# Gate and up products of an FFN by seven block products in place of eight, with sums of weight blocks formed on GpSimd

## Chip, cores and metric

The kernel runs on one core of a Trainium2 chip. The metric is the device time of one execution in microseconds (us), and shorter is better. TensorE (PE) multiplies matrices, VectorE (DVE) and ScalarE (ACT) work element by element, GpSimd (POOL) did little but issue transfers, and SyncE (SP) issues the loads of the big weights.

## The reference

Ten sublayers in a row over one sequence of 256 tokens with 1024 features, all in float32: an attention mixer, FFN, a Fourier mixer, FFN, then twice (FFN, token mixer, FFN). Six of the ten are FFNs, and the change touches these alone:

```python
def swiglu_2(h, w_in, w_out):
    gate, up = jnp.split(h @ w_in, 2, axis=-1)
    return (jax.nn.silu(gate) * up) @ w_out
```

`h` is the normed and modulated input, 256 x 1024. `w_in` holds gate and up weights, 1024 x 2816 each; `w_out` is 2816 x 1024. Each sublayer has a modulation (shift, scale, gate) which is a vector of 3072 numbers, the product of one row of 1024 numbers with a 1024 x 3072 matrix.

## The kernel before

**Layout.** Features lie on the partitions: `h` is 8 tiles of 128 x 256 (features x tokens). A weight tile of 128 x 128 is stationary in TensorE and the 256 tokens of `h` move through. One float32 matmul of the program shows as two records of MATMUL in the trace, so a count in a row is twice the count of the code's `mm` calls.

**An FFN.** The 2816 hidden features are 22 tiles. Tile n is unit n of the phase `w13`: gate (8 matmuls over the 8 feature tiles) and up (8 more) into the two halves of one PSUM bank `lin[n % 3]`. Two units come from one load of 2 MB (a block of `w13`, 11 to an FFN), 32 matmuls a block. ScalarE takes Silu of the gate half (L835), VectorE multiplies it by the up half and writes `big[:, n]` (L1422), features on the partitions, as the second product wants it. Then the phase `w2` makes 8 tiles of the result, 22 matmuls each (`project`), with VectorE adding each to `x` (`residual`, L1012).

In five of the six FFNs (sublayers 1, 3, 6, 7, 9, `folded`) the first 4 units (`RAW`) are made from the input before its norm is known (`raw_unit`), and VectorE scales them afterwards (`raw_scaled`, then L1416). From unit 4 on all six run alike, through `pairs`. Sublayer 4 runs all its units through `pairs`.

**Loads.** SyncE fills a ring of three slots of 2 MB, `ring`; a slot is loaded again when `s_unit` says that the units of its last block are summed.

**Modulation.** The matrices of later sublayers' modulations come in blocks of 0.5 MB (`ada`). GpSimd issues their loads (L464) into a ring of three slots, each after VectorE has used up the block three before (`s_ada_used`); VectorE reduces a block with one multiply-and-sum (L871). `ADA_PER_FFN` fixes how many blocks each FFN takes: 48, 48, 32, 32, 32, 0. Five eighths of them are spread over units 2 to 21, three eighths over the results of `w2`. This is VectorE's program order, written by hand:

```python
def ada(n):
    for _ in range(n):
        dve.wait_ge(s_ada_dma[m % ADA_SLOTS], ...)
        V.tensor_tensor_reduce(w, w, crow[...], ...).then_inc(s_ada_used, 1)
```

**Between the products.** TensorE waits for VectorE's multiply of unit 21 (`pe.wait_ge(*taken(unit0[s, "w2"] - 1))`) before the first matmul of `w2`.

**The engines' order.** Each engine executes its own list in order. A wait on a semaphore holds everything behind it on that engine.

Of the kernel before, what the change touches and what calls it, by code (L numbers as in the profile page):

```python
# [16 lines left out]
ALU = mybir.AluOpType  # L17
# [45 lines left out]
ADA_PER_FFN = [48, 48, 32, 32, 32, 0]  # L63

# [32 lines left out]
def build(nc, I, out, stop=10, dbg=None):  # L97
    subs = SUBS[:stop]
    with ExitStack() as ctx:
# [3 lines left out]
        def sem(name):  # L103
            return ctx.enter_context(nc.semaphore(name))
# [140 lines left out]
        s_squares_added = sem("squares_added")  # L245
        s_mixer_tables_dma = sem("mixer_tables_dma")
# [137 lines left out]

        def first_weights(n):
# [70 lines left out]
        def _(pool):  # L456
# [4 lines left out]
            for n in range(ADA_N * len(subs) - FIRST_GATE):  # L461
                if n >= ADA_SLOTS:
                    pool.wait_ge(s_ada_used, n - ADA_SLOTS + 1)
                pool.dma_start(ada_ring[n % ADA_SLOTS][:], I["ada"][n]).then_inc(s_ada_dma[n % ADA_SLOTS], 16)  # L464
# [3 lines left out]
        def _(act):  # L468
# [317 lines left out]
            for s, kind in enumerate(subs):  # L786
# [36 lines left out]
                if kind == "ffn":  # L823
                    u0 = unit0[s, "w13"]
                    for n in range(KF):
# [25 lines left out]
        def _(dve):  # L851
# [26 lines left out]
            def ffn_before(s):  # L878

                return subs[:s].count("ffn")  # L880
# [122 lines left out]
            def residual(s, name):  # L1003
# [6 lines left out]
                for m in range(KD):  # L1010
# [8 lines left out]
                    if name == "w2":  # L1019
                        ada(share(ADA_PER_FFN[ffn_before(s)] * 3 // 8, KD - 2, m))  # L1020
# [347 lines left out]
            for s, kind in enumerate(subs):  # L1368
# [37 lines left out]
                if kind == "ffn":  # L1406

                    ffn = subs[:s].count("ffn")
                    u0 = unit0[s, "w13"]
                    for n in range(KF):  # L1410
                        if folded(s) and n < RAW:
# [3 lines left out]
                            dve.wait_ge(s_silu, ffn * KF + n + 1)  # L1415
# [4 lines left out]
                        else:  # L1420
                            dve.wait_ge(s_silu, ffn * KF + n + 1)
# [14 lines left out]
        def _(pe):  # L1436
# [486 lines left out]
            for s, kind in enumerate(subs):  # L1923
# [15 lines left out]
                if kind == "ffn":  # L1939
# [166 lines left out]
```

## Time and profile before

| | |
|---|---|
| median of 3 runs | 2274.36 us (2272.35 to 2275.43) |
| the profiled execution | 2274.54 us |
| its span, first to last instruction | 2272.5 us |
| TensorE busy (matmul records) | 2211.6 us, 97% |
| VectorE, ScalarE, GpSimd busy | 34%, 16%, 5% |
| transfers | 438.27 MB, mean 193 GB/s |
| mean granted TensorE clock | 0.987 of full speed |

Times are those of one profiled execution. The 2.0 us between its span and its time are start and end of the program. "Busy" of a matmul group is the time covered by its records; the mean ns of one record is longer than the step from one to the next, because records overlap. "Idle before" is the time in which the engine did nothing just before instructions of the group, with what ended it.

### The profile page before, as it was taken

The page shows a single profiled execution, that of the slowest core. Times are in us where ns is not written, and L with a number is a line of the kernel's source. Part 1 is how long each engine was busy: PE and PEld are TensorE (multiplying, and loading weights), DVE is VectorE, ACT ScalarE, POOL GpSimd, SP SyncE. Part 2 cuts the span into 40 slices and gives each one's busy share as a digit, 9 for nine tenths or more (in the row PEclk, how much of TensorE's full clock was granted, in tenths as well). Part 3 has the DMA queues.
Part 4 walks back from the last instruction along what each step waited for, and adds up shares of the span by engine and source line. Part 5 has one row for each costly group of instructions (what it writes and reads, how often), then busy time and mean ns, then how long its engine had stood idle before and what let it go on. Part 6 is the DMA issues. An engine that isn't in the chain of part 4 may idle for free.

```text
span 2272.5 us, 23963 instructions
## 1 busy us (share of the span) xinstructions
PE 2211.6 (97%) x10232; PEld 1871.7 (82%) x10232; DVE 766.8 (34%) x1601; ACT 356.2 (16%) x667; POOL 118.8 (5%) x231
## 2 busy tenths in 40 slices
PE   7999999999999999999999999999999999999997
PEld 4777888868888888888788888888888868888886
DVE  6454333313334122336433422332233543340002
ACT  3233200022000100023140200020002223120001
POOL 0100011100111000100000000000010000000000
PEclk9999999999999999999999999999999999999998
DMA  9673576825767565643434465656564433444331
GB/s 357 226 259 102 213 267 245 311 79 186 270 248 295 220 230 199 254 147 146 162 111 148 157 231 200 236 195 231 213 231 154 154 148 111 148 148 148 137 127 70
DMA packets 61539, 438.27 MB, mean 193 GB/s; under 512 B 6976, under 2 KB 8768, under 8 KB 39552
## 3 DMA queue, kind: packets, MB, share of 16 engines
q1 hardware_dynamic: 28608, 318.35, 38.4%
q0 software_dynamic: 32256, 117.45, 13.9%
q8 instruction: 75, 1.23, 0.2%
q10 hardware_dynamic: 576, 1.05, 0.1%
q14 instruction: 24, 0.20, 0.0%
HBM read 434.72 MB, written 2.10 MB: 192 GB/s over the span
## 4 chain that ended last, share of the span: by engine, by line
PE 97%; DVE 1%; ACT 1%; issue 0%; DMA 0%; SPq 0%; ACTq 0%; DVEq 0%
PE lin L1460 79%; PE small_ps L1460 4%; PE lin L1775 2%; PE lin L1718 1%; PE small_ps L1794 1%; PE lin L1528 1%; PE lin L1732 1%; PE small_ps L1564 1%; PE small_ps L1685 1%; PE lin L1672 1%; PE lin L1740 1%; PE small_ps L1766 0%; PE pstat L1472 0%; PE lin L1600 0%; PE small_ps L1615 0%; PE lin L1587 0%
## 5 line engine op out<-in xcount | busy, mean ns | idle before, releaser
L1460 PE MATMUL lin<-h,ring 128*128 128x256 f32 x5424 | 1180.3, 380 | 5.4 <-ACT h L807 2.8
L1460 PEld LDWEIGHTS lin<-h,ring 128*128 128x128 f32 x5424 | 1030.0, 190 | 150.7 <-issue 9.2
L1460 PE MATMUL lin<-big,ring 128*128 128x256 f32 x2112 | 457.4, 379 | 7.9 <-DVE big L1422 7.9
L1460 PEld LDWEIGHTS lin<-big,ring 128*128 128x128 f32 x2112 | 400.8, 190 | 64.5 <-DVE big L1422 10.3
L871 DVE CUSTOM_DVE_ANT_0 ada_ring<-ada_ring,crow 128x1024 f32<-128x1024 f32 x224 | 268.2, 1219 | 26.7 <-DMA ada_ring<-in_ada 26.1
L1422 DVE TENSOR_TENSOR big<-sil,lin 128x256 f32<-128x256 f32 x112 | 47.1, 421 | 592.8 <-ACT sil L835 592.8
L464 POOL DMA_DIRECT2D ada_ring<-in_ada x224 | 118.3, 528 | 1592.9 <-DVE sums L871 1561.0
L1012 DVE SCALAR_TENSOR_TENSOR x<-lin,mod,x 128x256 f32<-128x256 f32 x80 | 38.7, 483 | 449.3 <-PE lin L1460 424.2
L835 ACT ACTIVATE sil<-lin 128x256 f32<-128x256 f32 x112 | 42.9, 383 | 723.2 <-PE lin L1460 723.2
L1460 PE MATMUL lin<-rec,ring 128*128 128x257 f32 (+1 forms) x608 | 148.2, 397 | 7.8 <-ACT rec L532 7.8
L1460 PEld LDWEIGHTS lin<-rec,ring 128*128 128x128 f32 x608 | 120.8, 199 | 28.5 <-issue 9.6
L1460 PE MATMUL small_ps<-rec,ring 128*128 128x257 f32 x448 | 102.0, 379 | 0.0
L1460 PEld LDWEIGHTS small_ps<-rec,ring 128*128 128x128 f32 x448 | 84.9, 189 | 12.5
L532 ACT ACTIVATE rec<-xc,modc 128x256 f32<-128x256 f32 x40 | 16.5, 496 | 353.8 <-DVE xc L934 353.8
L1775 PE MATMUL lin<-ring,h 128*128 128x512 f32 x128 | 56.7, 595 | 0.0
L1775 PEld LDWEIGHTS lin<-ring,h 128*128 128x128 f32 x128 | 23.7, 190 | 28.3 <-issue 28.3
L1304 DVE RECIPROCAL rec<-rec 128x1024 f32<-128x1024 f32 x2 | 13.1, 6552 | 55.9 <-ACT rec L775 55.9
L1321 DVE TENSOR_TENSOR att<-lin,big 128x512 f32<-128x512 f32 x16 | 11.1, 691 | 56.8 <-PE lin L1460 56.8
L1460 PE MATMUL lin<-yab,ring 128*128 128x256 f32 x128 | 30.2, 379 | 0.0
L1000 DVE RECIPROCAL rstd<-sd 128x256 f32<-128x256 f32 x10 | 17.5, 1753 | 33.1 <-ACT sd L508 33.1
L478 ACT ACTIVATE big<-lin 128x512 f32<-128x512 f32 x24 | 14.3, 596 | 89.4 <-PE lin L1460 80.6
L545 ACT ACTIVATE h<-xc,modc 128x256 f32<-128x256 f32 x56 | 28.2, 585 | 0.0
(296 smaller groups left out, 1175.1 us busy)
## 6 DMA issues: line engine op xcount, KB each, us to landing
ring<-in_w SPq DMA_DIRECT2D x66, 2048.0 KB, 8.3
ada_ring<-in_ada POOLq DMA_DIRECT2D x224, 512.0 KB, 5.6
ring<-in_w SPq DMA_DIRECT2D x48, 1408.0 KB, 6.1
ring<-in_gates SPq DMA_DIRECT2D x12, 2048.0 KB, 7.9
ring<-in_mproj SPq DMA_DIRECT2D x8, 2048.0 KB, 8.0
ring<-in_mtok SPq DMA_DIRECT2D x4, 2048.0 KB, 7.7
ring<-in_branch SPq DMA_DIRECT2D x4, 2048.0 KB, 7.8
ring<-in_wout SPq DMA_DIRECT2D x4, 2048.0 KB, 7.8
```

The source lines that it names most:

```text
L464: pool.dma_start(ada_ring[n % ADA_SLOTS][:], I["ada"][n]).then_inc(s_ada_dma[n % ADA_SLOTS], 16)
L545: A(h[:, k], xc[:, k], ACT.Identity, scale=fold_gain[:, k:k + 1], bias=fold_shift[:, k:k + 1]).then_inc(s_h_ready, 1)
L835: A(sil[:, n % 2], lin[(u0 + n) % NBANK][:, 0:T], ACT.Silu).then_inc(s_silu, 1)
L871: V.tensor_tensor_reduce(w, w, crow[:, 0 if s < FIRST2 else 1], 1.0, 0.0, ALU.mult, ALU.add, sums[:, s % 3, b:b + 1]).then_inc(s_ada_used, 1)
L1012: V.scalar_tensor_tensor(x[:, m], lin[(u0 + m) % NBANK][:, 0:T], mod[:, 16 + m:17 + m], x[:, m], ALU.mult, ALU.add).then_inc(s_taken_by_dv ...
L1422: V.tensor_tensor(big[:, n], sil[:, n % 2], lin[(u0 + n) % NBANK][:, T:2 * T], ALU.mult).then_inc(s_taken_by_dve, 1)
L1460: ins = mm(dst, w[:, lo:lo + m], rhs(k), start=k == 0, stop=k == nk - 1)
L1528: ins = mm(lin[i // 2][0:2, i % 2 * T:i % 2 * T + T], csil[:, 0:2, k], first_weights(n)[:, k * T:(k + 1) * T], start=k == 0, stop=k == KD - 1)
L1564: return nc.tensor.transpose(dst, src, ident[:])
L1672: mm(lin[n % NBANK][:], q, kh[:, a], start=True, stop=True).then_inc(s_logits, 1)
L1685: ins = mm(dst, vt[:, k, a * VD:(a + 1) * VD], pt[:, k], start=k == 0, stop=k == 3)
L1775: ins = mm(b[:], h[:, k, tt * P:tt * P + P], w[:, k * 512:(k + 1) * 512], start=k == 0, stop=k == KD - 1)
```

## The change

Tiles 0 to 3 of each FFN stay as they were. The other 18 tiles are made in 9 chunks of two tiles (one 2 MB block each), by a scheme that gets a product of 2 x 2 blocks from seven block products in place of eight. The 256 tokens are two halves, the 1024 features two halves, and the columns are the gate columns and the up columns of the chunk's two tiles. With A(i,k) for the quarters of `h` and B(k,j) for those of the weights, VectorE forms four sums of A once per FFN (`combine_h`), and GpSimd four sums of B in each chunk (`combine`: t1 = B12-B11, t2 = B22-t1, t3 = B22-B12, t4 = B21-t2, each 128 x 1024 elements).

Each of the seven products is 4 matmuls (`part`). Here a 128 x 128 tile of `h` or of its sums is stationary, and 256 columns of weights move; the result has tokens on its partitions. It lies in seven PSUM banks (`product_bank`). ScalarE copies two products to SBUF, VectorE makes nine operations of 128 x 256 a chunk out of the rest (`chunk`), and ScalarE applies Silu. Since `w2` wants features on the partitions, TensorE turns the hidden values with four 128 x 128 transposes a chunk (`turn_hidden`), and ScalarE copies them to `big`.

GpSimd now has the sums of weights and the issue of the modulation's loads in one list, with the loads of a chunk between t2 and t3. The modulation's blocks are placed anew: some before the first chunk, then 3, 3, 2, 2, 2, 0 after each chunk and after each of six results of `w2`. The first tile of `w2` begins before the last chunk's hidden values are turned.

```diff
+ADA_PER_CHUNK = [3, 3, 2, 2, 2, 0]
+ADA_PER_RESULT = [3, 3, 2, 2, 2, 0]
+CHUNKS = KF // 2 - RAW // 2
...
+def ada_before_chunks(f):
+    return ADA_IN_MLA + sum(ADA_PER_FFN[:f + 1]) - CHUNKS * ADA_PER_CHUNK[f] - (KD - 2) * ADA_PER_RESULT[f]
...
+def combined_weights(j, i):
+    place = ((proj[:, 0:4], proj[:, 4:8], proj[:, 8:12], proj[:, 12:16]),
+             (proj[:, 16:20], proj[:, 20:24], tok[:, 0:1], tok[:, 1:2]))[j % 2][i]
+    return place.rearrange("p a b -> p (a b)").rearrange("p (u kf) -> p u kf", u=2)
...
+def product_bank(s, n):
+    after = unit0[s, "w2"]
+    place = {1: pa[2], 2: pa[1], 3: pa[3], 5: pa[0], 6: lin[after % NBANK], 7: lin[(after + 1) % NBANK],
+             4: lin[(after + 2) % NBANK]}
+    return place[n][:, 0:T]
...
+    ada_issued = [0]
+    def ada_issue(used):
+        while ada_issued[0] < min(used + ADA_SLOTS, ADA_N * len(subs) - FIRST_GATE):
+            n = ada_issued[0]
+            ada_issued[0] += 1
+            if n >= ADA_SLOTS:
+                pool.wait_ge(s_ada_used, n - ADA_SLOTS + 1)
+            pool.dma_start(ada_ring[n % ADA_SLOTS][:], I["ada"][n]).then_inc(s_ada_dma[n % ADA_SLOTS], 16)
+    def combine(ph, f, j):
+        n, done = ph.first + RAW // 2 + j, f * CHUNKS + j - 1
+        if j >= 2:
+            pool.wait_ge(s_fourth_product, done)
+        pool.wait_ge(s_weights[n % SLOTS], (n // SLOTS + 1) * 16)
+        b11, b12, b21, b22 = [quarter(n % SLOTS, c, half) for half in range(2) for c in range(2)]
+        t1, t2, t3, t4 = [combined_weights(j, i) for i in range(4)]
+        W = nc.gpsimd.tensor_tensor
+        W(t1, b12, b11, ALU.subtract).then_inc(s_weights_combined, 1)
+        pool.wait_ge(s_weights_combined, nth(pool, s_weights_combined))
+        W(t2, b22, t1, ALU.subtract).then_inc(s_weights_combined, 1)
+        ada_issue(ada_before_chunks(f) + max(j - 1, 0) * ADA_PER_CHUNK[f])
+        W(t3, b22, b12, ALU.subtract).then_inc(s_weights_combined, 1)
+        pool.wait_ge(s_weights_combined, nth(pool, s_weights_combined))
+        W(t4, b21, t2, ALU.subtract).then_inc(s_weights_combined, 1)
+        nth(pool, s_weights_combined, 2)
+    for s, kind in enumerate(subs):
+        if kind == "ffn":
+            f = ffn_before(s)
+            ada_issue(ADA_IN_MLA + sum(ADA_PER_FFN[:f]))
+            pool.wait_ge(s_unit, unit0[s, "w13"] + 1)
+            for j in range(CHUNKS):
+                combine(by_name[s, "w13"], f, j)
+    ada_issue(ADA_N * len(subs))
...
+            for j in range(CHUNKS + 1):
+                if j < CHUNKS:
+                    act.wait_ge(s_first_product, nth(act, s_first_product))
+                    if j:
+                        act.wait_ge(s_first_up, nth(act, s_first_up))
+                    A(first_kept, product_bank(s, 1), ACT.Copy).then_inc(s_first_kept, 1)
+                if j:
+                    act.wait_ge(s_second_gate, nth(act, s_second_gate))
+                    A(second_gate, second_gate, ACT.Silu).then_inc(s_second_gate_silu, 1)
+                    act.wait_ge(s_hidden_turned, nth(act, s_hidden_turned))
+                    at = RAW + 2 * (j - 1)
+                    A(big[:, at:at + 2], pstat[:].rearrange("p (a b) -> p a b", a=2), ACT.Copy).then_inc(s_hidden_kept, 1)
+                if j < CHUNKS:
+                    act.wait_ge(s_first_gate, nth(act, s_first_gate))
+                    A(first_gate, first_gate, ACT.Silu).then_inc(s_first_gate_silu, 1)
+                    act.wait_ge(s_fifth_product, nth(act, s_fifth_product))
+                    if j:
+                        act.wait_ge(*taken(u0 + RAW + 2 * (j - 1) + 1))
+                    A(fifth_kept, product_bank(s, 5), ACT.Copy).then_inc(s_fifth_kept, 1)
+            nth(act, s_first_up)
...
+    def combine_h(s):
+        dve.wait_ge(s_h_ready, KD * (s + 1))
+        a11, a12, a21, a22 = [quarter_of_h(half, tt) for tt in range(2) for half in range(2)]
+        s1, s2, s3, s4 = [combined_h(i) for i in range(4)]
+        V.tensor_tensor(s1, a21, a22, ALU.add).then_inc(s_h_combined, 1)
+        V.tensor_tensor(s3, a11, a21, ALU.subtract).then_inc(s_h_combined, 1)
+        dve.wait_ge(s_h_combined, nth(dve, s_h_combined))
+        V.tensor_tensor(s2, s1, a11, ALU.subtract).then_inc(s_h_combined, 1)
+        dve.wait_ge(s_h_combined, nth(dve, s_h_combined, 2))
+        V.tensor_tensor(s4, a12, s2, ALU.subtract).then_inc(s_h_combined, 1)
+        nth(dve, s_h_combined)
+    def chunk(s, j):
+        def added(dst, a, b, signal=s_dve_chain):
+            V.tensor_tensor(dst, a, b, ALU.add).then_inc(signal, 1)
+            dve.wait_ge(signal, nth(dve, signal))
+        dve.wait_ge(s_second_product, nth(dve, s_second_product))
+        dve.wait_ge(s_first_kept, nth(dve, s_first_kept))
+        V.tensor_tensor(first_gate, product_bank(s, 2), first_kept, ALU.add).then_inc(s_first_gate, 1)
+        dve.wait_ge(s_sixth_product, nth(dve, s_sixth_product))
+        added(partial_2, product_bank(s, 6), first_kept)
+        dve.wait_ge(s_fifth_kept, nth(dve, s_fifth_kept))
+        if j:
+            dve.wait_ge(s_hidden_turned, nth(dve, s_hidden_turned))
+        added(first_up, partial_2, fifth_kept)
+        added(first_up, product_bank(s, 3), first_up, s_first_up)
+        dve.wait_ge(s_first_gate_silu, nth(dve, s_first_gate_silu))
+        V.tensor_tensor(first_up, first_up, first_gate, ALU.mult).then_inc(s_taken_by_dve, 1)
+        dve.wait_ge(s_seventh_product, nth(dve, s_seventh_product))
+        added(partial_3, product_bank(s, 7), partial_2)
+        dve.wait_ge(s_fourth_product, nth(dve, s_fourth_product))
+        V.tensor_tensor(second_gate, product_bank(s, 4), partial_3, ALU.add).then_inc(s_second_gate, 1)
+        added(partial_3, partial_3, fifth_kept)
+        dve.wait_ge(s_second_gate_silu, nth(dve, s_second_gate_silu))
+        V.tensor_tensor(second_gate, partial_3, second_gate, ALU.mult).then_inc(s_taken_by_dve, 1)
+        if j == CHUNKS - 1:
+            nth(dve, s_hidden_turned)
...
-                ada(share(ADA_PER_FFN[ffn] * 5 // 8, KF - 2, n - 2) if n > 1 else 0)
+                if n == 2:
+                    combine_h(s)
+            ada(ada_before_chunks(ffn) - ada_blocks[0])
+            for j in range(CHUNKS):
+                chunk(s, j)
+                ada(ADA_PER_CHUNK[ffn])
...
+    def gate_and_up(s):
+        ph, f = by_name[s, "w13"], ffn_before(s)
+        u0, before = ph.unit0, ffn_before(s) * CHUNKS
+        def part(product, activation, weight):
+            out = product_bank(s, product).rearrange("p (u f) -> p u f", u=2)
+            for k in range(4):
+                ins = mm(out, activation[:, k], weight[:, :, k * P:(k + 1) * P], start=k == 0, stop=k == 3)
+            return ins
+        def turn_hidden(j):
+            pe.wait_ge(*taken(u0 + RAW + 2 * j + 1))
+            if j:
+                pe.wait_ge(s_hidden_kept, before + j)
+            for a in range(2):
+                for tt, tokens in enumerate((first_up, second_gate)):
+                    at = a * T + tt * P
+                    ins = turn(pstat[:, at:at + P], tokens[:, a * P:(a + 1) * P])
+            ins.then_inc(s_hidden_turned, 1)
+        h_tile(KD - 1)
+        pe.wait_ge(s_h_combined, 4 * (f + 1))
+        for j in range(CHUNKS):
+            n = ph.first + RAW // 2 + j
+            slot_of(ph, 0, RAW // 2 + j)
+            b11, b12, b21, b22 = [quarter(n % SLOTS, c, half) for half in range(2) for c in range(2)]
+            t1, t2, t3, t4 = [combined_weights(j, i) for i in range(4)]
+            if j:
+                pe.wait_ge(s_first_gate, before + j)
+            else:
+                pe.wait_ge(*taken(u0 + 2))
+            part(1, quarter_of_h(0, 0), b11).then_inc(s_first_product, 1)
+            part(2, quarter_of_h(1, 0), b21).then_inc(s_second_product, 1)
+            if j:
+                turn_hidden(j - 1)
+                pe.wait_ge(s_first_up, before + j)
+            pe.wait_ge(s_weights_combined, 4 * (before + j + 1))
+            part(3, combined_h(3), b22).then_inc(s_unit, 2)
+            if j:
+                pe.wait_ge(s_fifth_kept, before + j)
+                pe.wait_ge(s_second_gate, before + j)
+            else:
+                pe.wait_ge(*taken(u0 + RAW - 1))
+            part(5, combined_h(0), t1).then_inc(s_fifth_product, 1)
+            part(6, combined_h(1), t2).then_inc(s_sixth_product, 1)
+            part(7, combined_h(2), t3).then_inc(s_seventh_product, 1)
+            part(4, quarter_of_h(1, 1), t4).then_inc(s_fourth_product, 1)
+        last = CHUNKS - 1
+        ph = by_name[s, "w2"]
+        w = slot_of(ph, 0, 0)
+        b = bank(ph.unit0)
+        def result(k0, k1):
+            for k in range(k0, k1):
+                if k >= RAW and k % 2 == 0:
+                    pe.wait_ge(s_hidden_kept, before + (k - RAW) // 2 + 1)
+                ins = mm(b[:, 0:T], w[:, k * P:(k + 1) * P], big[:, k], start=k == 0, stop=k == KF - 1)
+            return ins
+        pe.wait_ge(s_first_up, before + CHUNKS)
+        result(0, 16)
+        turn_hidden(last)
+        result(16, KF).then_inc(s_unit, 1)
...
-            for b in range(RAW // 2 if folded(s) else 0, ph.nb):
-                pairs(ph, b // SLOTS, b % SLOTS, 2, h_tile)
-            pe.wait_ge(*taken(unit0[s, "w2"] - 1))
-            project(s, "w2", lambda k: big[:, k])
+            if not folded(s):
+                for b in range(RAW // 2):
+                    pairs(ph, b // SLOTS, b % SLOTS, 2, h_tile)
+            gate_and_up(s)
+            ph = by_name[s, "w2"]
+            for m in range(1, KD):
+                w = slot_of(ph, m // SLOTS, m % SLOTS)
+                tile_sum(bank(ph.unit0 + m)[:, 0:T], w, 0, KF, lambda k: big[:, k]).then_inc(s_unit, 1)
```

## Rows read from the trace of the kernel before

**Rows 1.** The page: busy time and share of the span by engine; chain that ended last
```profile
PE 2211.6 (97%) x10232; PEld 1871.7 (82%) x10232; DVE 766.8 (34%) x1601; ACT 356.2 (16%) x667; POOL 118.8 (5%) x231
...
PE 97%; DVE 1%; ACT 1%; issue 0%; DMA 0%; SPq 0%; ACTq 0%; DVEq 0%
```

**Rows 2.** Chain in order of time (start us, us, what): FFN of sublayer 1, units 4 to 21, then w2
```profile
255.33 124.33 PE lin L1460 x576
380.92 76.24 PE lin L1460 x352
```

**Rows 3.** The chain between unit 21 and w2 in sublayer 1
```profile
379.66 0.02 issue
379.68 0.02 ACTq L834
379.70 0.04 issue
379.74 0.39 ACT sil L835
380.14 0.02 issue
380.16 0.43 DVE big L1422
380.59 0.33 issue
```

**Rows 4.** Chain elsewhere: transposes (L1564), 512 moving columns (L1775), 128 moving columns (L1794)
```profile
129.43 1.75 PE small_ps L1564 x16
...
1075.36 6.87 PE lin L1775 x16
...
1082.23 1.78 PE small_ps L1794 x16
```

**Rows 5.** Windows (units 4 to 21; w2): PE, PEld, DVE, ACT, POOL, PEclk, DMA share, GB/s
```profile
255.33:379.66 124.33, 124.32 (x576) 109.09 (x575) 39.41 (x76) 7.02 (x18) 14.25 (x27) 1.00 0.70 256
380.92:457.16 76.24, 76.24 (x353) 67.15 (x354) 26.02 (x48) 1.89 (x3) 10.56 (x20) 1.00 0.77 291
```

**Rows 6.** Groups of the whole trace on VectorE (busy us, mean ns | idle before)
```profile
L871 DVE CUSTOM_DVE_ANT_0 ada_ring<-ada_ring,crow 128x1024 f32<-128x1024 f32 x224 | 268.2, 1219 | 26.7 <-DMA ada_ring<-in_ada 26.1
...
L1422 DVE TENSOR_TENSOR big<-sil,lin 128x256 f32<-128x256 f32 x112 | 47.1, 421 | 592.8 <-ACT sil L835 592.8
...
L1234 DVE TENSOR_TENSOR xc<-rec 128x1024 f32<-128x1024 f32 x2 | 2.4, 1218 | 0.0
```

**Rows 7.** Groups of the whole trace on GpSimd: all that it writes itself, and its issues
```profile
L464 POOL DMA_DIRECT2D ada_ring<-in_ada x224 | 118.3, 528 | 1592.9 <-DVE sums L871 1561.0 <-DMA rec<-in_ada_pe 32.0
L457 POOL MEMSET ones<- 128x128 f32 x1 | 0.2, 205 | 0.3 <-POOLq L2097 0.3
...
L458 POOL MEMSET eps<- 128x1 f32 x1 | 0.1, 98 | 0.0
```

**Rows 8.** Timeline of sublayer 1 around unit 3's end (255.33): VectorE's chain to the first modulation block
```profile
257.23 0.48 DVE L1416 SCALAR_TENSOR_TENSOR big<-rec,small,sil 128x256 f32<-128x256 f32 x1 [0.98 <-ACT sil L830]
257.63 1.22 DVE L871 CUSTOM_DVE_ANT_0 ada_ring<-ada_ring,crow 128x1024 f32<-128x1024 f32 x1
258.78 0.08 DVE L871 DVE_READ_ACCUMULATOR2_ANT sums<- 128x1 f32 x1
258.78 1.22 DVE L871 CUSTOM_DVE_ANT_0 ada_ring<-ada_ring,crow 128x1024 f32<-128x1024 f32 x1
259.15 0.53 POOL L464 DMA_DIRECT2D ada_ring<-in_ada  x1 [6.71 <-DVE sums L871]
```

**Rows 9.** Windows, columns as in Rows 5: an idle stretch of TensorE and the stretch behind it
```profile
986.06:989.40 3.34, 0.70 (x3) 0.33 (x3) 2.69 (x7) 0.66 (x2) 0.00 (x0) 1.00 0.52 167
989.40:994.80 5.40, 5.40 (x17) 4.44 (x18) 1.62 (x3) 5.38 (x12) 0.00 (x0) 0.68 0.01 3
```

**Rows 10.** ScalarE: a copy of 512 columns out of PSUM, and where function tables are loaded
```profile
L478 ACT ACTIVATE big<-lin 128x512 f32<-128x512 f32 x24 | 14.3, 596 | 89.4 <-PE lin L1460 80.6 <-PE lin L1732 8.9
...
L508 ACT ACT_TABLE_LOAD x9 | 11.5, 1283 | 0.2
...
L830 ACT ACT_TABLE_LOAD x5 | 6.4, 1283 | 0.1
```

More of the change, by code:

```diff
@@ L245, in build @@
         s_squares_added = sem("squares_added")
+        s_weights_combined = sem("weights_combined")
+        s_h_combined = sem("h_combined")
+        s_first_product = sem("first_product")
+        s_second_product = sem("second_product")
+        s_fourth_product = sem("fourth_product")
+        s_fifth_product = sem("fifth_product")
+        s_sixth_product = sem("sixth_product")
+        s_seventh_product = sem("seventh_product")
+        s_first_kept = sem("first_product_kept")
+        s_fifth_kept = sem("fifth_product_kept")
+        s_first_gate = sem("first_gate")
+        s_first_gate_silu = sem("first_gate_silu")
+        s_first_up = sem("first_up")
+        s_second_gate = sem("second_gate")
+        s_second_gate_silu = sem("second_gate_silu")
+        s_hidden_turned = sem("hidden_turned")
+        s_hidden_kept = sem("hidden_kept")
         s_mixer_tables_dma = sem("mixer_tables_dma")
@@ L383, in raw_pair, with ffn_before, quarter, combined_h @@
             return rec[:, 12 + 2 * (r % 2):14 + 2 * (r % 2)]
+        def ffn_before(s):
+            return subs[:s].count("ffn")
+        def ada_before_chunks(f):
+            return ADA_IN_MLA + sum(ADA_PER_FFN[:f + 1]) - CHUNKS * ADA_PER_CHUNK[f] - (KD - 2) * ADA_PER_RESULT[f]
+        def quarter(slot, c, half):
+            return ring[slot][:].rearrange("p (u c k f) -> p u c (k f)", u=2, c=2, k=KD)[:, :, c, half * 512:half * 512 + 512]
+        def combined_weights(j, i):
+            place = ((proj[:, 0:4], proj[:, 4:8], proj[:, 8:12], proj[:, 12:16]),
+                     (proj[:, 16:20], proj[:, 20:24], tok[:, 0:1], tok[:, 1:2]))[j % 2][i]
+            return place.rearrange("p a b -> p (a b)").rearrange("p (u kf) -> p u kf", u=2)
+        def combined_h(i):
+            return sq[:, 2 * i:2 * i + 2].rearrange("p a b -> p (a b)").rearrange("p (k t) -> p k t", k=4)
+        def quarter_of_h(half, tt):
+            return h[:, 4 * half:4 * half + 4, tt * P:tt * P + P]
+        first_kept, fifth_kept, partial_2, partial_3, first_gate, first_up, second_gate = [att[:, i] for i in range(7)]
+        def product_bank(s, n):
[3 more added lines that the diff above has]
+            return place[n][:, 0:T]
         def first_weights(n):
@@ L460, in _ @@
             pool.wait_ge(s_ada_first_dma[FIRST_N - 1], 16)
[L461 to L464, printed above, removed]
+            ada_issued = [0]
[30 more added lines that the diff above has]
+            ada_issue(ADA_N * len(subs))
         @block.scalar
@@ L824, in _ @@
                     u0 = unit0[s, "w13"]
-                    for n in range(KF):
+                    f = ffn_before(s)
+                    for n in range(RAW):
                         if n >= 2:
@@ L1019, in residual @@
                     if name == "w2":
-                        ada(share(ADA_PER_FFN[ffn_before(s)] * 3 // 8, KD - 2, m))
+                        ada(ADA_PER_RESULT[ffn_before(s)] if m < KD - 2 else 0)
                 dve.wait_ge(*taken(u0 + KD - 1))
@@ L1406, in _ @@
                 if kind == "ffn":
-                    ffn = subs[:s].count("ffn")
+                    ffn = ffn_before(s)
                     u0 = unit0[s, "w13"]
-                    for n in range(KF):
+                    for n in range(RAW):
                         if folded(s) and n < RAW:
@@ L1414, in _ @@
                             dve.wait_ge(s_raw_scaled, nth(dve, s_raw_scaled))
-                            dve.wait_ge(s_silu, ffn * KF + n + 1)
+                            dve.wait_ge(s_silu, ffn * RAW + n + 1)
                             V.scalar_tensor_tensor(big[:, n], raw_pair(n)[:, 1], raw_shift(n, 1), sil[:, n % 2],
```

4 lines of the change are left out of this document (1 added, 3 removed).

## The prediction

> **What bounds the kernel now.** I read the page first: TensorE is busy 97% of the span and is 97% of the chain that ended last [rows 1]. So only what changes TensorE's list, or makes it wait, counts. Then the chain in order of time, at one FFN: units 4 to 21 run without a gap, 576 records in 124.33 us, or 0.216 us a record, and `w2` the same (352 records in 76.24 us) [rows 2]. A matmul of the code is two records, 0.432 us; a block of two tiles is 64 records, 13.8 us. The windows confirm it: TensorE has no idle time in either stretch, at full clock, with weight loads (PEld 109 of 124 us) under the matmuls [rows 5]. Between the two stands one gap of 1.26 us (379.66 to 380.92): Silu, multiply, and 0.33 us until TensorE starts [rows 3].
>
> **Part 1, the products.** Each chunk loses 4 of 32 matmuls of 256 columns, 8 records: 8 x 0.216 = 1.73 us. Over 9 chunks x 6 FFNs, **-93.2 us**. That weights move now changes no price: 16 records of 512 columns over stationary activations took 6.87 us [rows 4], 0.215 us for 256 columns. The moving operand is now two pieces of 128 columns, which no row shows; I take it at nothing, since one operand is read at the same width either way.
>
> **Part 2, the transposes.** Four a chunk. The trace has transposes at 16 records in 1.75 us and plain 128-column matmuls, with all 128 columns stationary, at 1.78 us [rows 4]: 0.111 us a record. 54 x 8 x 0.111 = **+48.0 us**. The floor is 0.109; the ceiling is a weight load of 109.09/575 = 0.190 us a record [rows 5] should loads not overlap, +82 us. I take 0.111: those rows ran back to back.
>
> **Part 3, the gap before `w2`.** The last chunk's chain now has 16 matmuls (6.9 us) of `w2` over it, and ScalarE's copy (0.60 us [rows 10]) of the turned values has four more. Six gaps of 1.26 us: **-7.6 us**.
>
> **Part 4, the turn in the steady chunk.** Let 0 be the end of a chunk's fourth product. TensorE goes on at once with products 1 and 2 of the next, 16 records, and is ready to turn at 3.29 (its records end 0.16 us after the next one begins). Against it runs a chain: ScalarE must first copy the next first product (end of the record 1.73, then 0.08 to start, 0.38), only then Silu (0.39), then VectorE's multiply 0.43 and 0.33 to TensorE [rows 3]: 1.73 + 0.08 + 0.38 + 0.02 + 0.39 + 0.02 + 0.43 + 0.33 = 3.4. I put 0.08 us on each of 48 turns, **+3.8 us**. ScalarE's two kinds of function don't alternate tables: loads stand on the lines of Sqrt and of the first Silu behind it, none on a copy [rows 10]. There is little slack here, so whatever holds VectorE moves TensorE.
>
> **Part 5, the first chunk.** Here the code makes a wait that nothing covers. Between t2 and t3 of chunk 0 GpSimd issues loads of modulation blocks, and each waits for a block to be used. VectorE uses these (3 in the first two FFNs, 2 in the next three, none in the last) only after unit 3's multiply. Product 3 waits for t4. From unit 3's end: multiply at +1.90, first block at +2.30, each further block 1.15 later, its load's issue 1.52 behind the block's start and 0.53 long [rows 8], then t3 and t4. For 3 blocks: 2.30 + 2.30 + 1.52 + 0.53 + 0.2 for the two handovers + 2T, less the 3.46 us of products 1 and 2: 3.39 + 2T. For 2 blocks 2.24 + 2T; in sublayer 4, whose multiply comes 0.5 after the unit, 0.79 + 2T. In all 12.05 + 10T.
>
> **T, one sum of 128 x 1024 on GpSimd**, has no row. VectorE does it in 1.22 us [rows 6]. GpSimd's own rows are memsets: 128 columns 0.205, one column 0.098 [rows 7], so 0.84 ns a column for one stream, 0.96 us for 1024. With two inputs and one output: 1.8 us if two streams take turns, 2.7 if three do. I take 2.3, between these; ends 0.96 and 2.7. Part 5 is then **+35.0 us** (21.7 to 39.1). For this size the Trainium skill (GPSIMD Engine Reference, Performance versus the Vector engine) gives 4497 ns for 2048 elements, 2.25 us for ours as an estimate; no row here shows it, and the sum by it would be 0.5 us less.
>
> After idle time TensorE's clock is lower for a while: 3.34 us nearly idle, then 5.40 us at a mean of 0.68 (part at the 1.2 GHz level), for 16 records that at full clock take 16 x 0.217 = 3.5, while the 1.26 us gap is followed by full clock (2.4 GHz) [rows 5, 9]. Five stalls of 5 to 8 us at 1.9: **+9.6 us**.
>
> Parts 1 to 5: -93.2 + 48.0 - 7.6 + 3.8 + 35.0 + 9.6 = **-4.4 us**. The saving is nearly spent before anything steady goes wrong.
>
> **Part 6, GpSimd's steady list.** A chunk takes TensorE 56 x 0.216 + 0.89 + 0.08 = 13.04 us. In it GpSimd needs 4T = 9.2 plus issues; alone it would fit, since a chunk's three issues end at 7.3 after the fourth product and t3, t4 at 11.9. But GpSimd and VectorE read the same memory, and VectorE has four operations a chunk with both inputs there (0.42 each) and the blocks (1.15 each). No row has both at work on such operands: GpSimd only issued loads, and those took 0.528 us whether VectorE was busy or not. My forecast is that they take turns, each waiting only its share: t1 and t2 4.6, 0.84 for two of VectorE's adds, a block amid them 1.15; the other two blocks then end at 8.9, the last issue at 9.8, and t3, t4 with 0.84 more give 15.2 us. With 2 blocks it is 14.1, with none 10.9. GpSimd then falls behind. Its first free chunk (9.4) and seven at 15.2 make 115.8 against TensorE's 8 x 13.04 = 104.3: 11.5 us in each of two FFNs; 9.4 + 7 x 14.1 - 104.3 = 3.8 in each of three. **+34.4 us**; ends 0 and the rival of full holding.
>
> **What costs nothing.** `combine_h`: four adds of 512 columns, some 2.8 us, behind unit 2, under unit 3's 6.9 us; uncovered it would cost that once an FFN. VectorE's nine operations replace two a block: 3.8 + 3.5 us of blocks, in 13. The transfers: a block and three modulation blocks are 3.7 MB in 13 us, 283 GB/s, and `w2` ran without a stall at 291 [rows 5]; a slot is freed at product 3, two chunks before its next block is needed.
>
> **Sum.** -4.4 + 34.4 = +30.0 on the profiled execution's 2274.54 (span 2272.5 and 2.0 around it), which is the median of 2274.36 within 0.2: **2304.5 us**.
>
> **Rivals.**
> - *No interference* (the other side). GpSimd's and VectorE's reads pass each other, part 6 is 0: 2274.5 - 4.4 = 2270.1. With T at 0.96 it is 2256.8, at 2.7 2274.1. It decides at T = 2.3: below it the kernel is faster. For it: 0.528 us issues beside busy VectorE. Against: issues read no tensor. Chance 0.29, of which 0.18 is faster by over 0.2%.
> - *Full holding at the turn.* An operation of either engine keeps the other's two-input operation out for its whole length. Then in part 4 VectorE's last multiply, ready at 2.6, meets t2, which runs from about 2.85 (t1 to 2.4, then VectorE's add) to 5.15. The turn begins at 5.15 + 0.43 + 0.33 = 5.9, not 3.3: 2.6 us x 48 = 125 us. Such a chunk is 15.6 us and hides GpSimd's 15.2, so part 6 goes: -4.4 - 3.8 + 125 = +117, **2391 us**. Against it: it needs GpSimd to start t1 before VectorE's add, 0.4 us after the product; if VectorE is first, the turn waits some 0.6 us and the blocks push GpSimd: about 2315, inside the forecast's part. Chance 0.25.
> - *Transposes at the weight loads' pace*: the ceiling of part 2, +34 on the forecast, 2339. Against it: both rows of part 2. Chance 0.05. This is the case in which fewer products bring no shorter work.
> - Forecast, shares of a conflict between nothing and full: 0.35, mostly 2280 to 2325. Rest 0.06, half of it faster.
>
> The page rule of the second rival is that of the Trainium skill (SBUF — State Buffer, Who interferes with whom): a VectorE instruction with two SBUF inputs contends with a GpSimd instruction that reads SBUF, and the later one waits for the whole of the earlier. It speaks against this change, and no run here shows it yet. By it the time is 2391; by the rows alone nothing excludes either it or the first rival.
>
> **Numbers.** The range reaches from the middle of the first rival to just past the second: 2260 to 2398. Outside lie T near 1 us, and stalls of 2.6 us that also lower the clock. Within 0.2% (4.5 us, about what a measurement of this kernel can tell from no change) is a third of the first rival: 0.10. Faster 0.21, slower 0.69.
>
> **What the next profile would show.** Parts 1 and 2: MATMUL records of `part` at 0.216 us a step, transposes at 0.11. Part 5: idle time of TensorE at product 3 of chunk 0 of 5 to 8 us in five FFNs, none in the last, released by GpSimd, with the clock below 1 after it. Part 6: waits at product 3 of later chunks, released by GpSimd, growing with the blocks per chunk and absent in the last FFN. The second rival: 48 waits of about 2.6 us before the transposes, released by VectorE, in the last FFN too. T: GpSimd's groups. If TensorE's idle time at chunk 0 is missing, or GpSimd's sums take under 1.5 us, I am wrong toward faster.

## The result, and the profile after

The kernel with the change takes 2346.51 us (median of 4 runs, 2344.92 to 2347.92) against 2274.89 before: ratio 1.0317, 95% interval [1.0299, 1.0334]. It is 72 us slower, where +30 was forecast. Line numbers (L...) shift by a few from run to run with the edits.

The page of the changed kernel, against [rows 1]:

```profile
span 2344.8 us, 24735 instructions
PE 2171.7 (93%) x10016; PEld 1823.1 (78%) x10016; DVE 1161.1 (50%) x2003; ACT 428.2 (18%) x829; POOL 630.5 (27%) x447
...
PE 82%; DVE 14%; issue 2%; POOL 1%; ACT 1%; DMA 0%; SPq 0%; DVEq 0%; ACTq 0%
```

TensorE is busy 39.9 us less (2211.6 to 2171.7), but idle 112.2 us more: 2344.8 - 2171.7 = 173.1, where it was 60.9. VectorE's busy time has grown by 394 us, and VectorE now holds 14% of the chain. Who TensorE waited for (us in total, times, longest):

```profile
PE pstat L1716 <- DVE att L1025: 79.0, 42, 2.3
PE small_ps L1726 <- POOL proj L542: 33.9, 5, 7.9
...
PE small_ps L1726 <- DVE sq L998: 6.6, 1, 6.6
```

The first is the turn (its transposes wait for VectorE's second multiply), the second product 3 of chunk 0, the third the sums of `h`. Together they are 119.5 us. The waits between unit 21 and `w2` are gone, which in the kernel before were:

```profile
PE lin L1460 <- DVE big L1422: 7.9, 6, 1.6
```

119.5 less 7.9 is 111.6, all but 0.6 of the new idle time. The groups of GpSimd and VectorE in a chunk (mean ns; [rows 6, 7] are before), and the transposes:

```profile
L536 POOL TENSOR_TENSOR proj<-ring 128x1024 f32<-128x1024 f32 x54 | 127.2, 2355 | 906.2 <-PE small_ps L1612 651.9 <-DMA ring<-in_w 130.1 <-PE lin L1726 99.1
L538 POOL TENSOR_TENSOR proj<-ring,proj 128x1024 f32<-128x1024 f32 x54 | 129.2, 2392 | 4.2
...
L1004 DVE TENSOR_TENSOR att<-att 128x256 f32<-128x256 f32 x108 | 177.6, 1645 | 1.9
L1004 DVE TENSOR_TENSOR att<-lin,att 128x256 f32<-128x256 f32 x108 | 45.6, 422 | 235.8 <-PE lin L1726 235.8
...
L1716 PE MATMUL pstat<-ident,att 128*128 128x128 f32 x216 | 35.7, 289 | 79.0 <-DVE att L1025 79.0
```

`att<-att` has both inputs in SBUF and takes 1645 ns on average; `att<-lin,att`, of the same size on the same line of code (that of a helper, `added`), has one input in PSUM and takes 422. The timeline of one turn in the last FFN, where VectorE has no modulation blocks (start us, us):

```profile
2207.97 2.35 POOL L536 TENSOR_TENSOR proj<-ring 128x1024 f32<-128x1024 f32 x1 [4.91 <-PE lin L1726]
2208.00 0.42 DVE L1022 TENSOR_TENSOR att<-lin,att 128x256 f32<-128x256 f32 x1 [1.37 <-PE lin L1726]
2208.34 2.27 DVE L1004 TENSOR_TENSOR att<-att 128x256 f32<-128x256 f32 x1
...
2209.94 0.41 ACT L934 ACTIVATE att<-att 128x256 f32<-128x256 f32 x1
2210.41 2.40 POOL L538 TENSOR_TENSOR proj<-ring,proj 128x1024 f32<-128x1024 f32 x1
2210.64 2.45 DVE L1025 TENSOR_TENSOR att<-att 128x256 f32<-128x256 f32 x1
...
2213.15 0.66 PE L1716 MATMUL pstat<-ident,att 128*128 128x128 f32 x4 [1.80 <-DVE att L1025]
```

The fourth product is there at 2207.9 and releases both engines. VectorE's add with a PSUM input runs beside t1. Its add with two SBUF inputs stands until t1 ends (2210.32) and ends 0.3 us later. The multiply, its Silu ready at 2210.35, stands behind t2. TensorE waits 1.80 us. This is the place and the order of the second rival. 35 of the 42 turns wait as long. In the two FFNs with three blocks a chunk seven others wait 2.27 us: there the multiply itself takes 0.43 us, but the operations ahead of it on VectorE have been held, by t3 and t4 and by the next t1 and t2, and it comes late.

**Where the 72.3 us of span come from:** products 432 x 0.216 = -93.2; transposes 216 x 0.111 = +24.0, and 0.22 us more at each of the 42 behind a wait (0.66 against 0.44 us for four; the end of the last record before a wait is covered by nothing), +9; the gap before `w2` -7.9; turns +79.0; chunk 0 +33.9; sums of `h` +6.6. That is 51.4; the other 21 us are records at a lower clock. The windows below (columns as in [rows 5]) lie behind the 7.9 us wait of the first chunk 0, behind a 2.27 us wait, behind another 2.27 us wait, behind the 6.6 us wait, and behind a 1.8 us wait:

```profile
265.90:271.41 5.51, 5.51 (x13) 4.43 (x14) 0.00 (x0) 0.00 (x0) 5.43 (x3) 0.50 0.24 45
298.72:302.13 3.41, 3.41 (x10) 2.65 (x9) 2.77 (x7) 0.76 (x2) 1.76 (x4) 0.50 0.36 103
674.60:680.00 5.40, 5.40 (x27) 4.83 (x28) 3.72 (x7) 1.38 (x3) 2.81 (x4) 1.00 0.47 170
2120.84:2124.86 4.02, 4.01 (x10) 3.21 (x11) 0.93 (x3) 0.73 (x2) 0.00 (x0) 0.50 0.07 24
2199.26:2202.71 3.45, 3.45 (x17) 3.04 (x17) 0.00 (x0) 0.90 (x2) 3.45 (x2) 1.00 0.41 76
```

At a granted clock of 0.50 (1.2 GHz) half of TensorE's time is lost. Stretches at 0.50 stand behind all five waits at chunk 0 (5.51, 4.89, 3.11, 3.68 and 4.04 us: 10.6 lost), behind five of the seven waits of 2.27 us (3.41 us each: 8.5 lost) and behind the sums of `h` (2.0 lost). These 21.1 us are the 21.

### The profile page after: what moved, and what is told of

It reads as the page before. It is cut to its first block, busy times and chain, and to the rows that moved or that the text cites. A ratio compares the mean times of both kernels' runs of the same rounds, so it can differ in the third digit from the quotient of the medians.

```text
span 2344.8 us, 24735 instructions
## 1 busy us (share of the span) xinstructions
PE 2171.7 (93%) x10016; PEld 1823.1 (78%) x10016; DVE 1161.1 (50%) x2003; ACT 428.2 (18%) x829; POOL 630.5 (27%) x447
## 4 chain that ended last, share of the span: by engine, by line
PE 82%; DVE 14%; issue 2%; POOL 1%; ACT 1%; DMA 0%; SPq 0%; DVEq 0%; ACTq 0%
PE lin L1612 42%; PE small_ps L1726 10%; PE lin L1726 9%; DVE att L1004 7%; DVE att L1025 4%; PE small_ps L1612 4%; PE lin L1776 2%; PE lin L1993 2%; PE pstat L1716 1%; PE lin L1936 1%; PE small_ps L2012 1%; DVE att L1022 1%; PE lin L1680 1%; PE lin L1950 1%; PE lin L1890 1%
## 5 line engine op out<-in xcount | busy, mean ns | idle before, releaser
L1612 PE MATMUL lin<-h,ring 128*128 128x256 f32 x1968 | 434.3, 382 | 5.4 <-ACT h L895 2.8
L1612 PEld LDWEIGHTS lin<-h,ring 128*128 128x128 f32 x1968 | 374.7, 191 | 60.6 <-issue 8.9
L536 POOL TENSOR_TENSOR proj<-ring 128x1024 f32<-128x1024 f32 x54 | 127.2, 2355 | 906.2 <-PE small_ps L1612 651.9
L1726 PE MATMUL small_ps<-ring,h 128*128 128x256 f32 x864 | 197.3, 382 | 6.6 <-DVE sq L998 6.6
L1726 PEld LDWEIGHTS small_ps<-ring,h 128*128 128x128 f32 x864 | 165.5, 192 | 29.8 <-issue 7.0
L1004 DVE TENSOR_TENSOR att<-att 128x256 f32<-128x256 f32 x108 | 177.6, 1645 | 1.9
L1726 PE MATMUL lin<-proj,sq 128*128 128x256 f32 x672 | 153.8, 379 | 0.0
L1726 PE MATMUL small_ps<-ring,sq 128*128 128x256 f32 x432 | 118.4, 423 | 33.9 <-POOL proj L542 33.9
L1726 PEld LDWEIGHTS lin<-proj,sq 128*128 128x128 f32 x672 | 127.7, 190 | 17.4
L538 POOL TENSOR_TENSOR proj<-ring,proj 128x1024 f32<-128x1024 f32 x54 | 129.2, 2392 | 4.2
```

The costliest lines, as they stand in the source:

```text
L536: W(t1, b12, b11, ALU.subtract).then_inc(s_weights_combined, 1)
L538: W(t2, b22, t1, ALU.subtract).then_inc(s_weights_combined, 1)
L1004: V.tensor_tensor(dst, a, b, ALU.add).then_inc(signal, 1)
L1612: ins = mm(dst, w[:, lo:lo + m], rhs(k), start=k == 0, stop=k == nk - 1)
L1726: ins = mm(out, activation[:, k], weight[:, :, k * P:(k + 1) * P], start=k == 0, stop=k == 3)
```

## The experiments

**1. t2 waits for the turn.** The changed kernel but for:

```diff
                 pool.wait_ge(s_weights_combined, nth(pool, s_weights_combined))
+                if j >= 2:
+                    pool.wait_ge(*taken(ph.unit0 + RAW + 2 * (j - 2) + 1))
                 W(t2, b22, t1, ALU.subtract).then_inc(s_weights_combined, 1)
```

> From chunk 2 on, GpSimd's t2 waits until VectorE's second multiply of the chunk two before is done, so that no sum of weights can lie over it. Theory A (a GpSimd operation that reads keeps VectorE's operations with two SBUF inputs out for its whole length): the 42 waits of 1.9 us before the transposes (79.0 us) and the slower records behind them (about 20 us of lower clock) go, but t2 now meets the modulation blocks, and the memory path has 4 x 2.37 + 4 x 0.42 + 3 x 1.15 = 14.6 us of work in a chunk with three blocks, 13.5 with two, 11.2 with none. So: the last FFN loses its waits wholly, the first two come to about 14.6 us a chunk in place of 15.6, in all 2285 us (2265 to 2310). Theory B (the turn is late because of the order of copies and Silu on ScalarE, not because of GpSimd): no change, 2346 us.

Measured: 2339.66 us, 1.0292 [1.0276, 1.0307]. The total was missed (2285 was expected, 2310 at most), the effect in the last FFN was not. Its chain, one chunk from product 3 to product 3 (start us, us; the first piece is products 3 and 5):

```profile
2200.39 3.46 PE small_ps L1728 x16
2203.85 5.18 PE lin L1728 x24
2209.03 3.45 PE small_ps L1728 x16
...
2212.92 3.46 PE small_ps L1728 x16
```

Chunks there come every 12.53 us and no turn waits; in the changed kernel they came every 14.55 (2198.60 to 2213.15). So the hold by t2 is what the turn waits for, and not ScalarE's order (theory B). In the FFNs with modulation blocks turns still wait:

```profile
PE pstat L1718 <- DVE att L1027: 61.7, 27, 3.6
```

There the same edit pushed t3, t4 and the next t1 together over VectorE's other adds:

```profile
288.82 2.37 POOL L542 TENSOR_TENSOR proj<-ring 128x1024 f32<-128x1024 f32 x1
289.13 6.95 DVE L1006 TENSOR_TENSOR att<-att 128x256 f32<-128x256 f32 x1 [0.37 <-ACT att L946]
...
291.13 2.36 POOL L544 TENSOR_TENSOR proj<-ring,proj 128x1024 f32<-128x1024 f32 x1
...
293.44 2.35 POOL L536 TENSOR_TENSOR proj<-ring 128x1024 f32<-128x1024 f32 x1
```

One add of 0.42 us stood through three GpSimd operations, 6.95 us, and the next turn waited 3.6. What the expectation had wrong was to count the path as a sum of work (14.6 us): VectorE doesn't get its turn between two GpSimd operations that follow each other directly (here they start 2.31 us apart and take 2.36), so a hold is longer than one operation. Between t1 and t2, where GpSimd first waits for t1's semaphore (2.44 us from start to start in the timeline above), the add did get in. The hold also goes the other way. A block's reduction that was under way held t2, which takes 2.39 us otherwise:

```profile
282.31 1.22 DVE L983 CUSTOM_DVE_ANT_0 ada_ring<-ada_ring,crow 128x1024 f32<-128x1024 f32 x1
282.54 3.21 POOL L540 TENSOR_TENSOR proj<-ring,proj 128x1024 f32<-128x1024 f32 x1 [0.89 <-DVE att L1027]
```

**2. Chunk 0's loads behind t4.**

```diff
-                ada_issue(ada_before_chunks(f) + max(j - 1, 0) * ADA_PER_CHUNK[f])
+                if j:
+                    ada_issue(ada_before_chunks(f) + max(j - 1, 0) * ADA_PER_CHUNK[f])
...
+                if j == 0:
+                    ada_issue(ada_before_chunks(f))
```

> In chunk 0 the loads of modulation blocks are issued behind t4, not between t2 and t3. If product 3 of chunk 0 waits for the loads' own waits: the five waits of 33.9 us in all and the slow records behind them (about 9 us) go, 2304 us. If GpSimd's late start only moves to chunk 1 or 2: over 2330 us, with waits at product 3 of a later chunk.

Measured: 2316.92 us, 1.0202 [1.0186, 1.0218], 29.6 us less than the changed kernel (28.3 if each is taken against its own measurement of before), and 13 over the 2304 expected. The wait for GpSimd is off TensorE's list altogether, and none came back at another product 3. TensorE's records take 6.9 us less (2171.7 to 2164.8). But the waits at the turns grew by 10 us:

```profile
PE pstat L1719 <- DVE att L1028: 89.1, 42, 4.1
```

So part 5 was a wait of the code's own making. It had the size that it was priced at, and a quarter of what its removal gave (33.9 + 6.9 us) went into longer turns.

**3. GpSimd writes, but doesn't read.** `W` is `nc.gpsimd.memset(dst, 0.01)`, so the sums of weights are left out.

> The four sums of weights are replaced by GpSimd memsets of the same tiles (0.96 us each expected), so the sums are left out and GpSimd writes but does not read. Theory A, reads alone collide: every VectorE operation of a chunk takes 0.42 us, no waits before the transposes over 0.2 us, product 3 of chunk 0 waits some 5 us, in all 2274.5 - 93.2 + 24 - 7.9 + 4 + 32 = 2234 us. Theory C, any GpSimd work on SBUF collides: VectorE's two-input operations of up to 1.3 us wherever a memset lies over them.

Measured: 2221.62 us in one run, 12 under the 2234 expected, which had put 32 us on chunk 0 and 4 on the turns (19.8 and 0 were measured). The memsets took 957 ns. VectorE's operations, min/median/max of the line that had 1645 ns:

```profile
L1005 DVE TENSOR_TENSOR att<-att x108: 415/420/426, 272.0 to 2124.9; 128x256 f32<-128x256 f32 x108
```

and at the place of the hold:

```profile
275.03 1.96 POOL L536 MEMSET proj<- 128x1024 f32 x2 [7.68 <-PE lin L1727]
275.07 0.42 DVE L1023 TENSOR_TENSOR att<-lin,att 128x256 f32<-128x256 f32 x1 [1.37 <-PE lin L1727]
275.42 0.42 DVE L1005 TENSOR_TENSOR att<-att 128x256 f32<-128x256 f32 x1
```

Memsets lie over VectorE's two-input add, and there is no hold. Reads collide and writes alone don't (theory A); theory C falls. Waits for GpSimd were left at chunk 0 alone (19.8 us), and no turn waited. VectorE has the same operations here as in the changed kernel, and this is its busy time:

```profile
PE 2147.2 (97%) x10016; PEld 1814.6 (82%) x10016; DVE 931.0 (42%) x2003; ACT 426.5 (19%) x829; POOL 320.1 (14%) x447
```

So of VectorE's 394 us more than before, 164 are its new operations and 230 are holds, recorded as busy time.

**4. GpSimd reads one operand.** `W` is `nc.gpsimd.tensor_copy(dst, a)`; the sums are left out again.

> Each sum of weights is replaced by a GpSimd copy of its first input, so the sums are left out; GpSimd reads one operand of 128 x 1024 and writes one. If any read keeps VectorE's two-input operations out, VectorE's att<-att operations again last up to the length of the copies that lie over them (longest over 1.2 us), and turns wait about the difference. If only GpSimd operations with two inputs do it, all stay at 0.42 us and the time is near that of the writes-only kernel, 2222 to 2240 us.

Measured: 2230.06 us in one run; a copy took 1065 ns.

```profile
L1005 DVE TENSOR_TENSOR att<-att x108: 415/426/932, 273.2 to 2133.4; 128x256 f32<-128x256 f32 x108
```

```profile
276.20 2.21 POOL L536 COPY proj<-ring 128x1024 f32<-128x1024 f32 x2 [7.83 <-PE lin L1727]
276.25 0.42 DVE L1023 TENSOR_TENSOR att<-lin,att 128x256 f32<-128x256 f32 x1 [1.37 <-PE lin L1727]
276.59 0.93 DVE L1005 TENSOR_TENSOR att<-att 128x256 f32<-128x256 f32 x1
```

The add under the first copy takes 0.93 us in place of 0.42: it ends 0.27 us behind the first copy. One input is enough to hold. "Over 1.2" was too much, for the add starts 0.4 us into the copy. No turn waited for these short holds. The time is 8.4 us over that of experiment 3, one run each, and no run isolated why.

**5. The hold by itself, in the kernel before.** After each of 24 loads of modulation blocks in the first FFN (waits that keep the 24 inside that FFN are left out here):

```diff
+                if 39 <= n < 63:
+                    flat = bias[:].rearrange("p a t c -> p (a t c)")
...
+                    nc.gpsimd.tensor_tensor(tok[:, 0], flat[:, 0:1024], flat[:, 1024:2048], ALU.subtract).then_inc(s_probe, 1)
```

> The kernel before, with 24 GpSimd subtractions of 128 x 1024 (two inputs in SBUF, result unused) put between the loads of modulation blocks in the first FFN; nothing else changed, no seven products. Theory A: VectorE's block reductions (two SBUF inputs) that meet one are held up to 2.4 us, longest near 1.22 + 2.3 = 3.5 us, while the multiplies with one input in PSUM stay at 0.42 us; TensorE has nothing behind them, so the time stays within 0.3% of before. If the long operations came from the new products' traffic, all of VectorE's operations keep their lengths.

Measured: 2272.12 us in one run beside 2273.84 before.

```profile
273.83 2.36 POOL L473 TENSOR_TENSOR tok<-bias 128x1024 f32<-128x1024 f32 x1
...
275.27 0.42 DVE L1432 TENSOR_TENSOR big<-sil,lin 128x256 f32<-128x256 f32 x1 [4.20 <-ACT sil L844]
275.61 1.67 DVE L880 CUSTOM_DVE_ANT_0 ada_ring<-ada_ring,crow 128x1024 f32<-128x1024 f32 x1
```

The multiply (one input in PSUM) takes 0.42 us in the middle of GpSimd's operation; the reduction that starts 0.58 us before its end takes 0.45 more than 1.22. Eight reductions were held so, all by the same 0.45, and no multiply took over 0.423. No seven products are there, so the hold doesn't come from them. The longest was far under 3.5, since VectorE reaches its blocks late in GpSimd's operation: how long a hold is depends on where in GpSimd's operation it starts.

**6. Edits 1 and 2 together.**

> The two edits together (t2 waits for the turn's multiply; chunk 0's loads behind t4). Theory A with the memory path as the bound of a chunk: the last FFN at 12.5 us a chunk, as the first edit alone gave, FFNs with two blocks 13.5 to 14.2 us, with three 15 to 15.6 us; in all 2339.7 less the 34 us of first-chunk waits and some clock, 2300 us (2290 to 2312). If the holds added nothing beyond the two places edited, it would come down to 2215.

Measured: 2308.45 us, 1.0158 [1.0143, 1.0174], inside the 2290 to 2312 expected. Turns still wait, fewer and longer:

```profile
PE pstat L1721 <- DVE att L1030: 69.8, 29, 3.7
```

In an FFN with two blocks a chunk the turns come every 14.4 to 15.3 us but for the last, more than the 13.5 to 14.2 expected: again the holds lie on the chain and don't fill gaps. None of the three placings of GpSimd's work tried here (experiments 1, 2 and 6) brings this division of work below before.

**7. The sums of weights on VectorE.** The seven products, turns and banks stay; GpSimd only issues loads. t1 and t2 of the chunk after next stand behind the modulation blocks, t3 of the next before the fourth product's add, t4 while ScalarE does the second Silu:

```diff
+            def weight_sum(s, j, i):
...
+                V.tensor_tensor(dst, a, b, ALU.subtract).then_inc(s_weights_combined, 1)
...
                 added(partial_3, product_bank(s, 7), partial_2)
+                weight_sum(s, j + 1, 2)
...
                 added(partial_3, partial_3, fifth_kept)
+                weight_sum(s, j + 1, 3)
...
                         ada(ADA_PER_CHUNK[ffn])
+                        for i in range(2):
+                            weight_sum(s, j + 2, i)
```

> The same seven products, but VectorE forms the sums of weights (1.22 us each), two behind the modulation blocks, one before the fourth product is there, one while ScalarE does its second Silu; GpSimd only issues loads. Theory A: nothing holds VectorE, whose own work is 3.8 + 3.5 + 4.9 = 12.2 us in a chunk of 12.6; the saving comes out: 2274.5 - 93.2 (products) + 24 (transposes) - 7.9 (gap before w2) + 4 (turns) + 5 (first chunks) = 2207 us; with VectorE the bound in the chunks with three blocks up to 2230. If the loss came from the products themselves (tokens on partitions, weights moving, seven banks), it stays at 2300 or more.

Measured: 2215.14 us, 0.9749 [0.9736, 0.9763]. Of its groups:

```profile
L998 DVE TENSOR_TENSOR proj<-ring,proj 128x1024 f32<-128x1024 f32 x84 | 102.9, 1225 | 2.9
...
L1003 DVE TENSOR_TENSOR att<-att 128x256 f32<-128x256 f32 x108 | 45.4, 420 | 7.6 <-DVE att L1003 4.3 <-ACT att L929 1.9
```

and of who TensorE waited for:

```profile
PE small_ps L1735 <- DVE sq L983: 14.3, 5, 2.9
```

Every operation has its own length again, and the products earn what they were priced at. VectorE is busy 1186.3 us, more than in the changed kernel (1161.1), and the turns' wait fell from 79.0 us to 0.8. The last row is the one miss, 8 us over the 2207 expected: chunk 0 waited for the sums of `h`, which I had put behind four sums of weights.

**8. Sums of `h` first.** In unit 2 `combine_h(s)` now stands ahead of the four `weight_sum(s, 0, i)` (in sublayer 4 these stood in unit 1).

> Sums of weights on VectorE as before, but the four sums of h are formed first, then those of chunk 0's weights. The kernel with the sums of weights ahead of them had five waits of TensorE of 14.3 us in all for the sums of h. They should go: 2215 - 14 - some 2 us of clock = 2200 us. If the fourth unit's multiply now comes too late for product 5, part of it stays, 2208 us.

Measured: 2200.14 us, 0.9673 [0.966, 0.9687]; measured again beside experiment 9, 2197.60, 0.9668 [0.9655, 0.9682]. The 14.3 us are gone, and of the waits before the transposes this is left:

```profile
PE pstat L1724 <- DVE att L1026: 3.7, 4, 1.5
```

**9. Second Silu first.** ScalarE does it before the copy of the next first product, and VectorE multiplies before t4.

> On top of the kernel with all sums on VectorE and those of h first (2200 us): ScalarE does the second Silu before it copies the next chunk's first product, and VectorE makes its second multiply before t4, so that the turn's chain no longer contains the first product. Its waits before the transposes were 3.7 us in all, and VectorE's list is 12.2 us of 12.5: at best 2196, within 0.2% of 2200; if VectorE's list is the bound, exactly no change. If t4 now comes too late for product 3, slower, 2205 or more.

Measured: 2197.33 us, 0.9667 [0.9653, 0.968], beside 2197.60 for experiment 8, which was measured again with it:

> The same kernel as the one with all sums on VectorE and those of h first, beside the one with the second Silu first, on the same chip, to compare the two: 2200 us again.

No difference. The turns' waits fell from 2.8 us (3.7 in the first measurement) to 0.7, and product 3 now waits 1.1 us for a sum of weights. The order on ScalarE is worth nothing here that the runs can tell.

## Why the prediction was wrong

The direction was right and the size was not: +72 us, forecast +30. The direction owes something to luck: the sum had +48.0 us for transposes that cost 24 and +34.4 for a GpSimd that made no wait, and these 58 us too many stood where the turns (79.0 against 3.8) belonged. That the result lies inside the range says little, for the range reached over both theories.

- **The step that failed is part 6**, "they take turns, each waiting only its share". There is no sharing. A GpSimd operation that reads SBUF keeps a VectorE operation with two SBUF inputs out to its end (experiments 4 and 5, with 3 as the case without reads), and operations of GpSimd in a row keep it out through all of them (experiment 1). GpSimd itself was hardly delayed in the changed kernel: its sums took 2.36 to 2.39 us on average and 2.53 at most, and product 3 waited for it only in chunk 0. So the +34.4 us of a late GpSimd were 0. The delay fell on VectorE, at the turn, which part 4 priced at 3.8 us with the remark that it had little slack: it cost 79.0 us, 9 in the transposes behind it, and 8.5 of clock. Without the holds the turn cost 0 (experiment 3) to 3.7 us (experiment 8), so part 4 was right as long as nothing held VectorE.
- **The second rival named the mechanism and the place**, given 0.25, and overpriced them: 2391. Its 2.6 us a turn were 1.8 to 2.3. From the end of the multiply to TensorE I had taken 0.33 us [rows 3], and it was under 0.1 (2213.09 to 2213.15); t2 also ran from 2210.41, 2.5 us behind the product, where I had it start at 2.85. And six of the 48 turns, the last but one of each FFN, have no t2 over them, since no chunk is left to prepare: the waits are 42. By 79.0 in place of 125, and with the transposes at 24.0, the rival's sum is -4.4 - 3.8 + 79.0 - 24.0 = +47, 25 us short of the result. The rule behind it (the Trainium skill, SBUF — State Buffer, Who interferes with whom) held here in what it says of the operands: two SBUF inputs on one side, a read on the other (1645 ns against 422 with one input in PSUM), and no hold under memsets. That the later one waits for the earlier held too, both ways, but for one thing: the add of 6.95 us in experiment 1 had waited since 289.13 and still came behind GpSimd operations that started at 291.13 and 293.44. I gave this rival less than the sharing that I found more moderate, and no row stood behind the sharing either.
- **Part 2** was mis-sized: I took two records for a transpose as for a matmul, and it is one (216 records for 54 x 4). 24.0 us, not 48.0. The row of transposes [rows 4] gives 16 records without saying how many transposes they are; the code would have told it.
- **Part 5** held: 33.9 us against 35.0, with T at 2.36 to 2.39 against the 2.3 taken between the bounds. Experiment 2 took it away. The price of the lower clock behind those waits held as well: 10.6 us against 9.6.
- **Parts 1 and 3** held: 0.216 us a record with weights moving, and -7.9 us. Experiments 3 and 7, where nothing is held, came to 2221.6 and 2215.1, with 19.8 and 14.3 us of waits at chunk 0 still in them. The sum of parts 1 to 3 with the true transposes is -93.2 + 24.0 - 7.9 = -77, and experiment 8 is 74 to 76 below before.
- **"`combine_h` costs nothing"** failed in the last FFN, by 6.6 us. There GpSimd's sums for chunk 1 (`tok` holds t3 and t4 of the odd chunks) came after a wait for their block, and lay over VectorE's scaling of `x`:

```profile
2106.63 8.84 DVE L1100 TENSOR_SCALAR x<-xc,top 128x256 f32<-128x256 f32 x8
2108.14 2.40 POOL L536 TENSOR_TENSOR proj<-ring 128x1024 f32<-128x1024 f32 x1 [5.80 <-DMA ring<-in_w]
2110.62 2.35 POOL L538 TENSOR_TENSOR proj<-ring,proj 128x1024 f32<-128x1024 f32 x1
2112.92 2.40 POOL L540 TENSOR_TENSOR tok<-ring 128x1024 f32<-128x1024 f32 x1
2115.28 2.39 POOL L542 TENSOR_TENSOR tok<-ring,proj 128x1024 f32<-128x1024 f32 x1
```

Eight operations that take 2.67 us in the four other FFNs of this kind took 8.84, up to the start of t4, and TensorE waited 6.6 us for `combine_h`. These have one tensor input in SBUF. That they were held by GpSimd is read from the timeline; no run isolated it.

No run changed the clock alone: the division of the 21 us is read from the granted clock of the changed kernel's trace. Why two of the seven waits of 2.27 us were followed by full clock stays open.

## What to carry to other kernels

Work moved to an idle GpSimd isn't free beside a VectorE that works on SBUF: before it is moved, list VectorE's operations with two SBUF inputs on a chain with little slack, and price each at the whole of the GpSimd operations that can lie over it. Here VectorE, at half the duration and with room in its list, did the same sums with 3.7 us of waits left at the turns, and a version 3.2% slower than before became one 3.3% faster. A wait inside a list that another engine's next step needs (loads between t2 and t3) is found by reading the code alone, and was worth 28 to 30 us.

## What the runs showed of the hardware that I had not expected

- One VectorE add of 0.42 us stood 6.95 us, through three GpSimd subtractions in a row. The profile counts this as busy time of VectorE: 1161 us against 931 for the same operations unheld (experiment 3) and 767 before. So the busy share holds 230 us that are no work, and a group whose mean (1645 ns) is far over that of its twin with a PSUM input (422) is the sign.
- GpSimd's subtraction of 128 x 1024 float32 took 2.36 to 2.39 us, its copy 1.07, its memset 0.96; VectorE's subtraction took 1.22.
- A float32 transpose is one record of 0.11 us, half the price of a matmul with 128 columns moving, which is two records of 0.111 us [rows 4].
- Behind none of the 35 waits of 1.8 us did TensorE's clock fall. Five of seven waits of 2.27 us were followed by 3.41 us at 0.50 (1.2 GHz), two by full clock. A wait of 7.9 us was followed by 5.51 us at 0.50.
